# A two-layer decoder trunk on one core: five small experts beside the big one, one left for the loop

## What is computed

```python
def moe_swiglu(h, w_router, w1, w3, w2):          # h: 256 tokens x 1024
    logits = (xt @ w_router)
    top_logits, top_idx = lax.top_k(logits, 2)
    gates = jax.nn.softmax(top_logits, axis=-1)
    ...
    # for each expert e and its tokens:
    yb = (silu(x_blk @ w1[e]) * (x_blk @ w3[e])) @ w2[e]    # 1024 -> 3584 -> 1024
    ...
    y = segment_sum(yb * gate, token)
```

## Time and profile before

| | us |
|---|---|
| three runs: median (lowest to highest) | 1749.46 (1746.77 to 1750.85) |
| the profiled execution | 1748.32 |
| its span | 1746.7 |
| TensorE busy (matmuls) | 1661.7 (95%) |
| TensorE weight loads | 1372.7 (79%) |
| VectorE busy | 1417.7 (81%) |
| ScalarE busy | 1048.8 (60%) |
| read from memory | 492.84 MB |

### The profile page before, as it was taken

One profiled execution on the slowest core, in us unless ns is written; L12 is line 12 of the kernel. 1 busy time (PEld: TensorE's weight loads), 2 busy tenths in 40 slices (PEclk: granted clock), 3 DMA queues, 4 the chain that ended last, 5 costly groups with the idle time before them and its releaser, 6 DMA issues.

```text
span 1746.7 us, 24307 instructions
## 1 busy us (share of the span) xinstructions
PE 1661.7 (95%) x8869; PEld 1372.7 (79%) x8869; DVE 1417.7 (81%) x1774; ACT 1048.8 (60%) x1303; POOL 56.9 (3%) x84
## 2 busy tenths in 40 slices
PE   5999988999999989999999999999999999999996
PEld 5988868999988878888767777777777777888875
DVE  4887676788878774798798989888887888988887
ACT  1544432434454444676677778776867787767774
POOL 0000000000000000100000000000000000010110
PEclk9998989999999899899999999999999999999998
DMA  9546555888845564798899989999998999999994
GB/s 307 163 145 193 198 167 189 282 277 278 262 133 181 157 217 145 282 387 309 304 339 350 370 318 369 355 340 349 362 357 332 359 382 366 346 379 368 365 389 166
DMA packets 270309, 503.74 MB, mean 288 GB/s; under 512 B 12646, under 2 KB 113272, under 8 KB 270200
## 3 DMA queue, kind: packets, MB, share of 16 engines
q1 hardware_dynamic: 262736, 489.72, 79.3%
q0 software_dynamic: 3072, 11.01, 1.8%
q10 hardware_dynamic: 4392, 1.57, 0.4%
HBM read 492.84 MB, written 9.44 MB: 288 GB/s over the span
## 4 chain that ended last, share of the span: by engine, by line
PE 47%; issue 42%; DVE 5%; POOL 1%; DMA 1%; ACTq 1%; POOLq 1%; ACT 1%; DVEq 0%; SPq 0%
PE ps L1913 10%; PE ps L1915 9%; PE ps L1914 9%; PE ps L2242 7%; PE ps L2241 6%; DVE lo_ring L1821 3%; PE ps L2378 3%; DMA weight_ring<-in_moe_w_dram 1%; PE ps L2205 1%; PE ps L2243 1%; POOL rstd L839 1%; DVE a_lo L1844 0%; DVE m_act L1840 0%; PE ps L2214 0%; POOL y_back L903 0%
## 5 line engine op out<-in xcount | busy, mean ns | idle before, releaser
L1821 DVE TENSOR_TENSOR lo_ring<-weight_ring,stage_hi 128x1024 fp32r<-128x1024 f32 x420 | 487.6, 1219 | 78.8 <-ACT stage_hi L1182 76.8
L1182 ACT CAST stage_hi<-weight_ring 128x1024 fp32r<-128x1024 f32 x420 | 415.1, 1051 | 32.1 <-DMA weight_ring<-in_moe_w_dram 31.0
L1564 DVE TENSOR_TENSOR lo_ring<-weight_ring,stage_hi 128x1024 fp32r<-128x1024 f32 x252 | 292.0, 1218 | 19.5 <-ACT stage_hi L1111 18.9
L1111 ACT CAST stage_hi<-weight_ring 128x1024 fp32r<-128x1024 f32 x252 | 247.1, 1052 | 43.1 <-DMA weight_ring<-in_moe_w_dram 40.8
L1313 DVE TENSOR_TENSOR lo_ring<-weight_ring,stage_hi 128x2048 fp32r<-128x2048 f32 x81 | 184.8, 2291 | 72.3 <-ACT stage_hi L975 64.7
L1913 PE MATMUL ps<-h_hi,stage_hi 128*128 128x256 f32 x800 | 233.7, 292 | 8.8 <-DVE h_lo L1276 7.0
L1914 PE MATMUL ps<-h_lo,stage_hi 128*128 128x256 f32 x800 | 229.9, 287 | 0.0
L1915 PE MATMUL ps<-h_hi,lo_ring 128*128 128x256 f32 x800 | 229.7, 287 | 0.0
L975 ACT CAST stage_hi<-weight_ring 128x2048 fp32r<-128x2048 f32 x81 | 153.5, 1905 | 123.0 <-DMA weight_ring<-in_w_in_dram 61.8
L1913 PE MATMUL ps<-stage_hi,xe_hi 128*128 128x512 f32 x448 | 182.0, 406 | 4.1 <-DVE lo_ring L1564 2.5
L1915 PE MATMUL ps<-stage_hi,xe_lo 128*128 128x512 f32 x448 | 176.9, 395 | 0.0
(11 more groups left out here) (379 smaller groups left out, 2624.8 us busy)
## 6 DMA issues: line engine op xcount, KB each, us to landing
weight_ring<-in_moe_w_dram SPq DMA_DIRECT2D x336, 1024.0 KB, 7.5
weight_ring<-in_w_mod_dram SPq DMA_DIRECT2D x48, 1024.0 KB, 6.0
weight_ring<-in_w_in_dram SPq DMA_DIRECT2D x36, 1024.0 KB, 5.5
weight_ring<-in_ffn_w_dram SPq DMA_DIRECT2D x33, 1024.0 KB, 6.4
weight_ring<-in_w_out_dram SPq DMA_DIRECT2D x12, 1024.0 KB, 4.9
moe_rows<-y_moe POOLq DMA_DIRECT2D x6, 512.0 KB, 5.2
moe_rows<-y_e POOLq DMA_DIRECT2D x3, 512.0 KB, 7.8
x_tok<-in_x_dram SPq DMA_DIRECT2D x1, 1024.0 KB, 10.9
```

Of the source, the lines that this page charges most:

```text
L1111: nc.scalar.copy(jst_hi[i % JSTAGES][:, part], ring[:, n % RING, part]).then_inc(hi_ready, 1)
L1182: nc.scalar.copy(jst_hi[g % JSTAGES][:, part], ring[:, n % RING, part]).then_inc(hi_ready, 1)
L1564: nc.vector.tensor_tensor(ring_lo[:, n % RING, part], ring[:, n % RING, part], raw(jst_hi[i % JSTAGES][:, part]), ALU.subtract).then_inc(l ...
L1821: nc.vector.tensor_tensor(ring_lo[:, n % RING, part], ring[:, n % RING, part], raw(jst_hi[g % JSTAGES][:, part]), ALU.subtract).then_inc(l ...
```

## The change

The group takes five small experts instead of four, the loop one instead of two. COL_RANK, the columns and the rows for the results move accordingly, and a fifth extra column keeps the room for experts that overflow. The group has 252 slots instead of 210; the numbers of small slots behind each big slot are new. `sT`, `silu`, `act`, `hi`, `lo`, `rows` and `sum` are placed by the same rules as before.

```diff
-EXTRA = 4
+EXTRA = 5
-COL_RANK = [NE - 1, 0, 0, 3, 4, 5, 6, 1, 2]
-COL_BIG, COL_SMALL, COL_LOOP = 1, 3, 7
+COL_RANK = [NE - 1, 0, 0, 2, 3, 4, 5, 6, 1]
+COL_BIG, COL_SMALL, COL_LOOP = 1, 3, 8
 NCOL = len(COL_RANK) + EXTRA
 SMALL = 64
-NSMALL = 4
+NSMALL = 5
...
-        behind = [3, 1 if ch == 0 else 3, 6, 6, 3, 3] if ch < NCH - 1 else [6, 6, 6, 6, 2, 0]
+        behind = [4, 2 if ch == 0 else 4, 7, 7, 4, 4] if ch < NCH - 1 else [7, 7, 7, 7, 4, 0]
...
-PLACES_C = 22
+PLACES_C = 29
...
-        epick = m("epick", [P, NCOL, NE])
+        epick = pick[:, 1]
...
-                nc.vector.tensor_scalar(step1[:], place[:], 1.0, 6.0 * P, ALU.is_ge, ALU.mult)
-                nc.vector.tensor_scalar(step_few[:], place[:], 3.0, -6.0 * P, ALU.is_ge, ALU.mult)
-                nc.vector.tensor_scalar(step7[:], place[:], 7.0, -7.0 * P, ALU.is_ge, ALU.mult)
+                nc.vector.tensor_scalar(step1[:], place[:], 1.0, 7.0 * P, ALU.is_ge, ALU.mult)
+                nc.vector.tensor_scalar(step_few[:], place[:], 2.0, -6.0 * P, ALU.is_ge, ALU.mult)
+                nc.vector.tensor_scalar(step7[:], place[:], 7.0, -8.0 * P, ALU.is_ge, ALU.mult)
```

More of the change, by code:

```diff
@@ L1676, in more_jobs @@
                 nc.vector.drain()
-                nc.vector.tensor_tensor(epick[:], ohk[:], iota[:, 0:NE].unsqueeze(1).to_broadcast([P, NCOL, NE]), ALU.mult)
+                nc.vector.tensor_tensor(epick, ohk[:], iota[:, 0:NE].unsqueeze(1).to_broadcast([P, NCOL, NE]), ALU.mult)
                 nc.vector.tensor_tensor(pick[:, 0, new], ohk[:, new], cap[:].unsqueeze(1).to_broadcast([P, EXTRA, NE]), ALU.mult)
```

## The result

The changed kernel takes 1773.1 us (median, 1769.5 to 1776.5) against 1749.3 for the kernel before, a ratio of 1.0141 with a 95% interval of 1.0125 to 1.0157: 24 us slower. The prediction said 1778, slower. The profiled execution took 1771.98 us, its span is 1770.3, 23.6 more than the kernel before.

What follows compares the result with a forecast made beforehand. TensorE was taken to bound the group and loop: -25.9 us saved, +52.8 of new waits and +3 for the rest make +29.9 on 1748.3, so 1778 us, range 1755 to 1812.

Steps and rivals of the forecast that it cites:

- TensorE paces the group, the gain is 26 us: In the group TensorE sets the pace; moving one expert saves 25.9 us; without new waits the group needs 727.0 us.
- 28 bare folds: In the group, 28 of 35 folds have no big-expert slot directly behind them to hide TensorE's wait.
- Their price: Waits behind the group's bare folds: 41.6 for the product, 6.8 behind gathers, 4.4 at the last fold; 52.8 us.
- lower bound of 38.8: Total of the group's new waits, in us, if all 23 waits for the product cost only 1.2 us.
- fourteen called usual: Bare folds with no big slot between last `w3` slot and fold, VectorE behind: 2.2 us each, 30.8 us.
- nine called quick: Bare folds with a big slot between last `w3` slot and fold, VectorE ahead: 1.2 us each, 10.8 us.
- The rest, +3: Late weights in runs of seven small slots and one possible low-clock stretch, between -4 and +10, taken as +3 us.
- The signs: Expected in the profile: the new waits, a group of about 780 us; wrong if 2.9 us a slot or clock 0.5 inside.
- Stream: Rival: weight transfers set the group's pace and waits hide; +4.7 us, 1753 us; chance 5%.
- Low clock: Rival: TensorE drops to 1.2 GHz behind bare folds in the group; 1810 us, or 1826 if all 28; chance 15%.
- Faster: Rival: VectorE catches up at folds, so new waits replace 20.1 us of old weight-load waits; -7.2 us, 1741 us; 5%.
- Overflow: Rival: the moved expert has above 64 tokens, so a second loop turn runs; +121.6 us, 1900 us; chance 2%.

Runs made afterwards that it cites:

- e1: Changed kernel with the small-slot numbers reordered so that a slot of the big expert follows every fold; 1733.3 us, ratio 0.9917 to the kernel before.
- e2: Kernel before, four small experts, only the order shifted by one small slot so that no big slot follows any of the 28 folds; 1821.5 us, ratio 1.0412.
- e3: Changed kernel plus four matmuls into an idle bank behind each bare fold that nothing else follows; 1769.6 us, ratio 1.0130 to the kernel before.
- e7: e2 plus four matmuls into an idle bank behind each bare fold that nothing else follows; 1804.2 us, ratio 1.0318 to the kernel before.
- e4: Changed kernel with silu, product, cast and remainder of bare folds one slot earlier on ScalarE and VectorE; 1792.5 us, ratio 1.0264 to the kernel before.
- e8: Kernel before with three more clearing transfers of 0.5 MB each, 1.5 MB in all; 1752.6 us, ratio 1.0024.

## Why the prediction was right, step by step

- **TensorE paces the group, the gain is 26 us.** That the order on TensorE decides is shown from both sides: e1 gains 14 us over the kernel before with five experts, e2 loses 74 with four. The whole 26 didn't come in e1. By its trace 13.3 us stay in the group beyond the plain sum and 4.9 in the first expert; a first issue 4.0 us earlier, and 4.4 us less from the last group issue to the last issue, give some back: -25.9 + 13.3 + 4.9 - 4.0 - 4.4 = -16.1, on a span 15.9 shorter.
- **28 bare folds.** Right: 23 waits on the product, four behind gathers, one on the last.
- **Their price.** Forecast 41.6 + 6.8 + 4.4 = 52.8 us. Measured, with 0.17 a restart: 25.3 + 23 x 0.17 = 29.2; 4.9 + 0.7 = 5.6; 4.13 + 0.17 = 4.3. Together 39.1, at the lower bound of 38.8. The term that was mis-sized is that of the 23 waits for the product, 41.6, and in it the fourteen called usual: 30.8 forecast, 16.2 measured. The nine called quick came to 13.1, forecast 10.8. Two steps failed. First, I priced every one of the 23 from the fold on, but behind six of the fourteen the big expert's transposes (`bT`) stand before `w1` and cover 0.9 us, as at 1130 us:

```profile
1130.47 1.04 PE L2386 MATMUL ps<-ident,m_act 128*128 128x128 f32 x8
1131.92 0.51 PE L2241 MATMUL ps<-stage_hi,sx 128*128 128x512 f32 x1 [0.41 <-DVEq L1829]
```

  These six cost 0.58 each, restart included, where 2.2 was taken: 9.7 us of the difference. Second, the rule for quick and usual ones doesn't hold. Of the nine with a big slot between the last `w3` slot and the fold, five waited 0.96 us and four (chunks 5, 10, 15, 25) 1.68. Of the other eight, without transposes, six waited 1.20 and two 1.97 and 2.16, and with the 0.17 the six lie 0.83 each under the 2.2: 5.0 us. How far VectorE is behind at a fold can't be read off the list of slots by this rule. That each wait lets VectorE get ahead, which I had named but not priced, would explain the smaller ones, but is not shown: in e2, with as many waits, they are 1.84 on average.
- **The rest, +3.** It came to 11: 3.3 in the first expert (taken as 0 to 1; the clearing transfers meet the weights where the DMA engines are full, and I had called them covered), 1.3 behind the last fold (5.6 at the end of the group less the wait's 4.3; the clock is low there), and in the group 768.4 - 727.0 - 34.8 = 6.6. In these lie the seven stretches at the low clock (e3 brought back 3.7 us with five of them) and some 0.1 us more for each of the 27 waits: idle time is counted from the modelled end of the matmul before, but from start to start a quick one takes 1.23 us where 0.09 is usual behind a fold, and its restart 0.11 more, 1.25 in all and not 0.96 + 0.17. The sum with what was measured, -25.9 + 39.1 + 3.3 + 1.3 + 6.6 - 0.9 (the earlier start) = 23.5, closes on the 23.6 of the spans. Forecast were 29.9: 14 too much for the waits, 8 too little for the rest. That these partly cancel is luck; the total is nearer than its terms. The bounds, too, were looser than they look: 38.8 and 98.6 give 1764 and 1824 us, and the 1800 given with the chances isn't worked out from them.
- **The signs.** The 23, four and one waits came as said, though six of the 23 are 0.41 and not 1 to 2. The group was to take about 780 us at 3.1 a slot, with less than 345 GB/s, and took 765.4 at 3.05, with 345. One of the signs of being wrong came: the clock does show 0.5 inside the group, seven times. It was too strict a sign, since by e3 the clock costs some 5 us at most.
- **The rivals.** Stream: out by e1, which brings the same transfers 28 us sooner. The rule of the Trainium skill set beside it ("Perfetto Trace Analysis", Identifying the Most-Contended Engine) pointed to the weights in the prediction's reading (weight loads busy 74.5%, 353 GB/s), and yet TensorE's order decides. Low clock: its mechanism is real and worth 17 us in the kernel with all folds bare (e2, e7), but here only a few (e3). What I had set against it, that the clock held through a wait of 1.7 us, was one wait. And that the trace before shows a low clock at the seam alone holds for its group and loop; from 700 to 730 us, in the first expert, its mean is 0.78. Faster: the late weights of the earlier trace rows did shrink, from 4.4 us to 1.4 for the matmuls, but more was never to be had from them than that. Overflow: the loop turned once.

## What to carry to other kernels

In a schedule written out by hand, list for every wait which work stands between the producer and the waiting instruction, before and after: here new numbers in one list took the cover of 5.7 us from 28 folds, and putting it back turned a loss of 24 us into a gain of 14 (1733 us, the best version). When the number of items changes, keep the phase of the cover, not the shape of the list. And moving the dependent steps earlier was no remedy here (e4): they held up the independent work behind them on the same engine.

## What the runs showed of the hardware that I hadn't expected

- TensorE's granted clock fell to 1.2 GHz again and again behind short waits: 15 times in e2, 14 of them in the group (once every 50 us), mostly for 3.41 us. All waits for the product there but one (3.9 us) are under 2.6 us, and all but two stand directly behind a fold's 16 matmuls of 64 columns. Filling 0.93 us of 24 waits with matmuls took nine of the fifteen away and 17 us with them.
- With the product one slot earlier, all 17 plain waits behind a fold are 0.96 us (e4): the chain of silu and product by itself. With the two slots of the changed kernel they run from 0.96 to 2.16.
- 1.5 MB of writes of zeros beside weight transfers at 390 GB/s went with a first expert 3.8 us longer, about their full transfer time (e8, one trace).
